# Four edits to a decoder step on eight cores: order of the first loads, spills as rows are done, conv weights in halves, all last down tiles segment by segment

## The reference, cut to what matters

```python
def decoder_layer(x, ...):
    x = x + 0.5 * swiglu_ffn(rms_norm(x, ffn1_norm), ffn1_w_gu, ffn1_w_down)
    mix, ... = token_mixer(rms_norm(x, mix_norm), conv_prev, ...)
    x = x + mix
    x = x + 0.5 * swiglu_ffn(rms_norm(x, ffn2_norm), ffn2_w_gu, ffn2_w_down)
# swiglu_ffn: gate, up = split(x @ w_gu); (silu(gate) * up) @ w_down
# rms_norm:   x * rsqrt(mean(x*x) + eps) * g
# token_mixer: spatial gating branch + (GLU, depthwise conv of width 31, layer norm, silu) branch, gated, one output projection
y = rms_norm(x, final_norm)
```

## Time and profile before

| | us |
|---|---|
| median of 3 runs | 3295.9 (3292.66 to 3832.61) |
| the profiled execution | 3292.83 |
| its span, first to last instruction, slowest core (7) | 3291.3 |
| spans of the eight cores | 3272.9 to 3291.3 |
| PE busy | 3188.5 (97%) |
| DVE busy | 1303.8 (40%) |
| ACT busy | 518.5 (16%) |

### The profile page before, as it was taken

One profiled execution on the slowest core, in us unless ns is written; L12 is line 12 of the kernel. 1 busy time (PEld: TensorE's weight loads), 2 busy tenths in 40 slices (PEclk: granted clock), 3 DMA queues, 4 the chain that ended last, 5 costly groups with the idle time before them and its releaser, 6 DMA issues.

```text
span 3291.3 us, 52487 instructions; the slowest of 8 cores (3272.9 to 3291.3 us)
## 1 busy us (share of the span) xinstructions
PE 3188.5 (97%) x21434; PEld 2052.3 (62%) x21434; DVE 1303.8 (40%) x2368; ACT 518.5 (16%) x957; POOL 128.1 (4%) x246
## 2 busy tenths in 40 slices
PE   6999999999999899999999999999999999999995
PEld 3566666666666576688666666666666666666662
DVE  2433333333336476675642222234333333333345
ACT  2200100000015122245111011033100100100121
POOL 0000000000000000000000000000000000000000
PEclk7999999999999899999999999999999999999997
DMA  6435624335336655534434433482434334434333
GB/s 164 77 58 102 108 52 84 70 56 89 70 62 163 120 115 119 120 82 93 87 56 78 77 70 64 73 186 52 90 62 86 68 59 86 73 59 81 72 62 109
DMA packets 75213, 284.38 MB, mean 86 GB/s; under 512 B 10977, under 2 KB 37857, under 8 KB 53090
## 3 DMA queue, kind: packets, MB, share of 16 engines
q0 software_dynamic: 34848, 216.62, 37.4%
q1 hardware_dynamic: 40130, 64.41, 6.7%
HBM read 468.13 MB, written 32.89 MB: 152 GB/s over the span
## 4 chain that ended last, share of the span: by engine, by line
PE 93%; DMA 3%; DVE 3%; issue 1%; ACT 1%; DVEq 0%; SPq 0%; ACTq 0%; POOLq 0%
PE ps L201 93%; DVE arena L207 1%; DVE arena L214 1%; DMA arena<-xin 1%; DMA cst<-arena 1%; DMA arena<-xsp 1%; DMA arena<-w_glu 1%; DMA arena<-w_gu 1%; DVE arena L218 0%; ACT arena L204 0%; ACT L204 0%; DVE arena L210 0%; DVEq L1138 0%; DVE arena L221 0%; SPq L1147 0%
## 5 line engine op out<-in xcount | busy, mean ns | idle before, releaser
L201 PE MATMUL ps<-arena 128*128 128x384 bf16 (+5 forms) x21434 | 3188.5, 311 | 88.7 <-ACT arena L204 26.3
L201 PEld LDWEIGHTS ps<-arena 128*128 128x128 bf16 x21434 | 2052.3, 98 | 1224.6 <-issue 115.8
L204 ACT ACTIVATE arena<-arena 128x384 f32<-128x384 f32 (+7 forms) x780 | 412.0, 550 | 2563.1 <-DVE arena L207 2405.8
L207 DVE TENSOR_TENSOR arena<-ps,arena 128x384 f32<-128x384 f32 (+2 forms) x504 | 270.4, 538 | 774.7 <-PE ps L201 752.9
L207 DVE TENSOR_TENSOR arena<-arena 128x384 f32<-128x384 f32 (+12 forms) x682 | 461.0, 688 | 283.0 <-ACT arena L204 249.5
L214 DVE SCALAR_TENSOR_TENSOR arena<-ps,arena 128x384 f32<-128x384 f32 (+6 forms) x452 | 241.7, 537 | 414.9 <-PE ps L201 414.1
L207 DVE TENSOR_TENSOR arena<-arena,ps 128x384 bf16<-128x384 f32 (+6 forms) x488 | 225.9, 477 | 393.7 <-PE ps L201 374.0
L1147 POOL DMA_DIRECT2D arena<-w_gu x88 | 46.6, 530 | 1160.2 <-PE ps L201 1131.7
L204 ACT ACTIVATE arena<-ps,arena 128x272 bf16<-128x272 f32 (+4 forms) x148 | 69.8, 487 | 134.8 <-PE ps L201 131.2
L1147 POOL DMA_DIRECT2D arena<-w_dn x64 | 33.8, 528 | 772.4 <-PE ps L201 772.4
L218 DVE RECIPROCAL arena<-arena 128x384 f32<-128x384 f32 (+4 forms) x14 | 36.6, 2613 | 51.3 <-ACT arena L204 51.3
(11 more groups left out here) (9 smaller groups left out, 8.0 us busy)
## 6 DMA issues: line engine op xcount, KB each, us to landing
arena<-w_gu POOLq DMA_DIRECT2D x88, 1024.0 KB, 9.2
arena<-w_dn POOLq DMA_DIRECT2D x64, 704.0 KB, 7.2
arena<-w_glu POOLq DMA_DIRECT2D x16, 1024.0 KB, 10.1
arena<-w_gate POOLq DMA_DIRECT2D x16, 1024.0 KB, 9.0
arena<-w_pab POOLq DMA_DIRECT2D x16, 1024.0 KB, 10.1
arena<-w_v POOLq DMA_DIRECT2D x8, 1024.0 KB, 8.8
arena<-w_u POOLq DMA_DIRECT2D x8, 1024.0 KB, 8.0
arena<-w_out POOLq DMA_DIRECT2D x8, 1024.0 KB, 11.1
```

The costliest lines, as they stand in the source:

```text
L201: return P.op("pe", lambda e: e.matmul(out, lhsT, rhs, start=start, stop=stop), deps)
L204: return P.op("act", lambda e: e.activation(out=out, in_=in_, func=func, **kw), deps)
L207: return P.op("dve", lambda e: e.tensor_tensor(out=out, in0=in0, in1=in1, op=op), deps)
```

## The change

What it does:

1. *Prelude.* All four loads of segment 0 are issued at once. The hook is called before a weight tile is issued and gives a wait for it: tile 1 waits for segment 0's group 2, tile 2 for segment 1's group 1, tile 3 for segment 2's group 0. Segment 1's loads wait for segment 0's last one, segment 2's for segment 1's last. In `units_by_row` the gate parts of all tiles come before the up parts.
2. *Spill.* Rows 0 to 3, 4 to 7 and 8 to 9 are stored as soon as they are done (hook "m"), rows 10 to 15 as before.
3. *Conv weights.* Each is a list of two halves, run one after each `glu_unit`; the memsets and the first weights stand behind block 0 of the held blocks.
4. *Last group of the second FFN.* `dn_seg` is 8: all eight down tiles are held and run segment by segment. Four are in the slots, four more go to `spare`, the place of H2, by DMAs on POOL that wait for the last gate/up matmul. `direct` is 12 for segment 0 and 6 for the others (before: 10).
5. *Final norm.* ACT multiplies X by the gain in place behind each row's Square. `finish` only does `root`; `last_rows` gives four steps, each one DVE tensor_tensor of 4 rows (128x1536 or 128x1280) by RSTD and the store of these rows. Segment s - 1's steps run behind rows 2, 4, 6 and 8 of segment s, the last segment's at the end.

```diff
@@ -266,7 +266,7 @@
 ev_pv = P.dma("sp", PV, pv_d, "c_pv")
-load_tokens(0, (0, 1))
+load_tokens(0, range(4))
@@ -327,7 +327,10 @@
         self.pend.append((k, si, sq[:, 0:n], act(sq[:, 0:n], X, AF.Square, deps=[dep] + sfree)))
-        if self.Hout is not None:
+        if self.Hout is None:
+            self.out[(self.s, k)] = act(X, X, AF.Identity, deps=[self.pend[-1][3], ev_pv],
+                                        scale=pvc(self.gidx, k))
+        else:
@@ -360,24 +363,31 @@
-    def finish(self, on_pool=()):
+    def finish(self):
         self.flush()
-        er = root(self.bank, self.lm, self.x0, self.n)
-        self.rout[self.s] = er
-        if self.Hout is None:
-            n, s = self.n, self.s
-            for k in range(KC):
-                X = self.Xs[s][:, k, 0:n]
-                R = RSTD[:, self.x0:self.x0 + n]
-                self.out[(s, k)] = stt(X, X, pvc(self.gidx, k), R, ALU.mult, ALU.mult, deps=[er, ev_pv],
-                                       eng="dve")
+        self.rout[self.s] = root(self.bank, self.lm, self.x0, self.n)
+    def last_rows(self):
+        if self.Hout is not None:
+            return []
+        x0, n, s = self.x0, self.n, self.s
+        def rows(g):
+            def run():
+                X = self.Xs[s][:, 4 * g:4 * g + 4, 0:n]
+                e = tt(X, X, RSTD[:, x0:x0 + n].unsqueeze(1).to_broadcast([128, 4, n]), ALU.mult,
+                       deps=[self.rout[s], self.out[(s, 4 * g + 3)]])
+                P.dma("sp", y_o[:, 4 * g:4 * g + 4, x0:x0 + n], X, "o_y", deps=[e])
+            return run
+        return [rows(g) for g in range(4)]
...
-def ffn(segs, Hv, HID, Xs, hready, rstd, norms, dn_seg, x_final, hook, first):
+def ffn(segs, Hv, HID, Xs, hready, rstd, norms, dn_seg, x_final, hook, first, spare=()):
@@ -429,8 +439,9 @@
         tok.finish()
-        for (jj, slot, lev), ((gi_, bg, _f), (ui_, bu, _h)) in zip(tiles, got):
-            up_part((ui_, bu), last[jj][1], jj, s, gate_part((gi_, bg), last[jj][0], s))
+        gps = [gate_part((gi_, bg), last[jj][0], s) for (jj, slot, lev), ((gi_, bg, _f), _u) in zip(tiles, got)]
+        for (jj, slot, lev), (_g, (ui_, bu, _h)), gp in zip(tiles, got, gps):
+            up_part((ui_, bu), last[jj][1], jj, s, gp)
@@ -450,11 +461,10 @@
                 if not wahead:
-                    wissue()
+                    wissue(hook("w", jj))
                 held.append(wnext())
-                hook("w", jj, held[jj][2])
             if not wahead:
-                wissue()
+                wissue(hook("w", 3))
@@ -485,12 +495,20 @@
             wdone(wi, [ld])
+            if gi == 3:
+                hook("m", mp)
...
             for mp in range(nm, 8):
-                held.append((mp,) + wnext())
+                if len(held) < 4:
+                    held.append((mp,) + wnext())
+                else:
+                    src, n = wseq.pop(0)
+                    buf = spare[len(held) - 4]
+                    held.append((mp, None, buf, P.dma("pool", buf, src, "wx%d" % mp, deps=norms[0].hdep)))
             for s in range(3):
+                steps = norms[s - 1].last_rows() if s > 0 else []
@@ -502,9 +520,12 @@
                         if s > 0 and m == 16 - 2 * dn_seg:
-                            norms[s - 1].finish(range(8, 16))
-                    if s == 2:
+                            norms[s - 1].finish()
+                        elif m % 2 == 0:
+                            run_steps(steps, 1)
+                    if s == 2 and wi is not None:
                         wdone(wi, [ld])
+                run_steps(steps, 99)
@@ -521,7 +542,9 @@
     if what == "w":
-        load_tokens(i, (2, 3) if i == 0 else range(4), [ev])
+        if i in (1, 2):
+            load_tokens(i, range(4), [x_ev[(i - 1, 3)]])
+        return [] if i == 0 else [x_ev[((0, 2), (1, 1), (2, 0))[i - 1]]]
@@ -546,15 +569,13 @@
         cst["wp"] = P.dma("pool", WP, wp_d, "c_wp")
-    if what == "g" and i == 3:
-        m1 = 16 - 2 * DN_SEG
+    if what == "m" and i % 2 == 1 or what == "m" and i == 7 - DN_SEG:
+        m0, m1 = 4 * (i // 2), 2 * i + 2
         for s in range(3):
-            sp_ev[(s, 0)] = P.dma("sp", xsp[s][:, 0:m1, :], X1[s][:, 0:m1, :], "xsa%d" % s,
-                                  deps=[x1f[(s, m1 - 1)]])
+            P.dma("sp", xsp[s][:, m0:m1, :], X1[s][:, m0:m1, :], "xsp%d" % s, deps=[x1f[(s, m1 - 1)]])
     if what == "s":
-        m1 = 16 - 2 * DN_SEG
-        sp_ev[(i, 1)] = P.dma("sp", xsp[i][:, m1:16, :], X1[i][:, m1:16, :], "xsb%d" % i,
-                              deps=[x1f[(i, 15)]])
+        m0 = 16 - 2 * DN_SEG
+        sp_ev[i] = P.dma("sp", xsp[i][:, m0:16, :], X1[i][:, m0:16, :], "xsp%d" % i, deps=[x1f[(i, 15)]])
@@ -655,23 +676,29 @@
 def conv_weights(c):
-    wp = WP[:, c]
-    e = None
-    for h in range(2):
-        e = tt(WD[c % 2][:, 2 * h:2 * h + 2].rearrange("p g b (i c) -> p (g b i) c", c=32),
-               MSKC.unsqueeze(1).to_broadcast([128, 72, 32]),
-               wp[:, 72 * h:72 * h + 72].unsqueeze(2).to_broadcast([128, 72, 32]), ALU.mult,
-               deps=[cst["wp"]] + wd_free[c % 2] + x1_dead)
-    return e
+    def half(h):
+        def run():
+            built[c] = h + 1
+            cw[c] = tt(WD[c % 2][:, 2 * h:2 * h + 2].rearrange("p g b (i c) -> p (g b i) c", c=32),
+                       MSKC.unsqueeze(1).to_broadcast([128, 72, 32]),
+                       WP[:, c, 72 * h:72 * h + 72].unsqueeze(2).to_broadcast([128, 72, 32]), ALU.mult,
+                       deps=[cst["wp"]] + wd_free[c % 2] + x1_dead)
+        return run
+    build.extend([half(0), half(1)])
+build = []
+built = {}
+cw = {}
...
 cg = {}
-cw = {}
 def conv(c):
+    while c not in cw or built[c] < 2:
+        run_steps(build, 1)
@@ -732,21 +759,24 @@
                 x1_dead = [hm[(0, 15)], hm[(1, 15)], hm[(2, 15)]] + list(sp_ev.values())
+                e_ph = memset(PHM, 0.0, deps=x1_dead)
+                for i in range(4):
+                    e_ph = memset(PHM[32 * i:32 * i + 32, i, :], 1.0, deps=[e_ph])
+                conv_weights(0)
+                conv_weights(1)
+            else:
+                run_steps(build, 1)
...
     cg[c] = conv_cache(c)
-e_ph = memset(PHM, 0.0, deps=x1_dead)
-for i in range(4):
-    e_ph = memset(PHM[32 * i:32 * i + 32, i, :], 1.0, deps=[e_ph])
-cw[0] = conv_weights(0)
-cw[1] = conv_weights(1)
...
         la = glu_unit(c, slot, lev, s)
+        run_steps(build, 1)
@@ -756,7 +786,7 @@
         if cc + 2 < KC:
-            cw[cc + 2] = conv_weights(cc + 2)
+            conv_weights(cc + 2)
@@ -1102,20 +1132,17 @@
 yf = {}
-normf = [RowNorm(PV_FIN, X2, None, SEG_B, s, yf, {}, SQF, ACCF[s], 10, PARTS[s]) for s in range(3)]
+normf = [RowNorm(PV_FIN, X2, None, SEG_B, s, yf, {}, SQF, ACCF[s], (12, 6, 6)[s], PARTS[s]) for s in range(3)]
...
-ffn(SEG_B, H2, HID2, X2, h2, r2, normf, 3, x3f, hook2,
+spare = [view(OFF_US + i * 5632, [2816], BF16) for i in range(4)]
+ffn(SEG_B, H2, HID2, X2, h2, r2, normf, 8, x3f, hook2,
     [(0, [0], None, norm2[2].finish), (0, [1, 2], None, None), (1, [0, 1, 2], None, None),
-     (2, [0, 1, 2], None, None)])
-normf[2].finish(range(11, 16))
-for s in range(3):
-    x0, n = SEG_B[s]
-    for g in range(4):
-        P.dma("sp", y_o[:, 4 * g:4 * g + 4, x0:x0 + n], X2[s][:, 4 * g:4 * g + 4, :], "o_y",
-              deps=[yf[(s, 4 * g + q)] for q in range(4)])
+     (2, [0, 1, 2], None, None)], spare)
+normf[2].finish()
+run_steps(normf[2].last_rows(), 99)
```

More of the change, by code:

```diff
@@ L211, in ts, with stt @@
                                                          op0=op0, op1=op1), deps)
-        def stt(out, in0, scalar, in1, op0, op1, deps=(), eng="dve"):
-            return P.op(eng, lambda e: e.scalar_tensor_tensor(out=out, in0=in0, scalar=scalar, in1=in1,
+        def stt(out, in0, scalar, in1, op0, op1, deps=()):
+            return P.op("dve", lambda e: e.scalar_tensor_tensor(out=out, in0=in0, scalar=scalar, in1=in1,
                                                                 op0=op0, op1=op1), deps)
@@ L1058, in build_program @@
                                     xsp[s][:, 4 * mg:4 * mg + 4, 0:SEG_B[s][1]], "xr%d_%d" % (s, mg),
-                                    deps=[lya, lyb, lgb, sp_ev[(s, 0)], sp_ev[(s, 1)]])
+                                    deps=[lya, lyb, lgb, sp_ev[s]])
         x2f = {}
```

## The result

The changed kernel takes 3258.2 us (median of 4 runs, 3257.5 to 3258.85) against 3294.3: a ratio of 0.9892, 95% interval 0.9873 to 0.9912. It is 36 us faster, 1.1%, where 46.9 us (1.4%) were forecast. That is less than the 2% which the forecast took as the mark of a change, as it said; by the interval it is a gain.

The account below looks back on a forecast made before the run. The prediction took the kernel as bound by matmuls (PE busy 3188.5 of 3291.3 us). 18.8 + 3.4 + 6.5 + 18.2 = 46.9 us off 3292.8 gave 3246, 3249 for the median; range 3236 to 3267, its own 3238 to 3258.

Parts of the forecast that it names:

- rival B: Prelude bound by the chain of loads, tile 1 at 36 us or later: 10 us less gain, 3259; chance 0.18.
- C: Rival: a new wait at the end, from late extra tiles or DVE falling further behind: 3257 to 3265; chance 0.17.
- Part 1: Prelude: reordered loads 17.5 us, gate products ahead of ups about 1.3 us; 18.8 us off.
- the chain: Prelude: tile 0 near 15 us, segment 0 in at 21.5, tile 1 near 30.5, PE goes on at 38.6.
- Part 2: Spill: without the store burst ahead of the GLU tiles, 2 us less wait and 1.4 of slow matmuls; 3.4 off.
- Part 3: Conv weights: wait of 9.35 us ahead of the first block falls by 6.2, cool-down by 0.3; 6.5 off.
- the cores draw together: Conv weights: the slowest core gets this gain and the quickest less; no size given.
- Parts 4 and 5: Last group and final norm: PE's waits of 2.95, 11.56 and 10.56 us go, smaller ones come; 18.2 us off.
- The extra tiles: Last group: four more down tiles land at 11.5 to 24.5 us, just in time, so no wait.
- E: Rival: the extra tiles cost more than everything else gives, from 47 us of wait on them; chance 0.02.
- The tail: Kernel's end: four steps replace 16 products, so stores start earlier; 1.1 to 1.9 us off.
- Each restart: PE's matmuls behind a long wait run partly at the lower clock level: 1.5 us charged each time.

Follow-up runs that it names:

- e2: The kernel before with the spill's edit alone (rows 0 to 9 stored as they are done): ratio 0.9988.
- e7: The changed kernel with the last of three GLU tiles held until the second has landed: ratio 0.9888 to the kernel before.
- e5: The changed kernel with one more half of the conv weights built behind conv block 1: 3252.9 us.
- e8: The changed kernel with weight tile 1 waiting for segment 0's second load instead of its third: ratio 0.9882 to the kernel before.

## Why the prediction was right, and where it was wrong

**Direction, verdict and range**: right, 3258.2 lies in 3236 to 3267, at the edge of the forecast's own range of 3238 to 3258. The size was 1.3 times the measured one, and 9.7 of the 10.8 us of difference lie in one place, the middle. The time alone would speak as well for rival B (3259) or C (3257 to 3265); the lines speak against both, as tile 1 came before 36 and the last group has no wait over 3.4 us.

**Part 1, right in the chain and the total, in part by luck.** 18.8 forecast, 17.7 measured (14.2 on core 3). The chain was as worked out: first load at 8.1 us, segment 0 in at 22.7, tile 1 behind the third load. But each step came later than in the sum, tile 0 at 17.6 in place of 15, and segment 1's by-row start at 40.6 in the mean over the cores, not 38.6: 14.6 us earlier than before, not 17.5. What made up for it was no term of the sum: the 112 matmuls behind that start took 18.36 us, where they had taken 20.3 in the mean (granted clock 1.00 on core 3, 0.89 on core 7 before). POOL's timeline of the changed kernel, core 3:

```profile
21.35 0.53 POOL L1174 DMA_DIRECT2D arena<-w_gu  x1 [19.13 <-DMA arena<-xin]
38.81 0.53 POOL L1174 DMA_DIRECT2D arena<-w_gu  x1 [16.93 <-DMA arena<-xin]
```

Tile 1 was issued at 21.35, not 18.5, and took 12.4 us; the sum had 12. On core 6 it was issued at 19.58 and PE started on it at 30.25. The Trainium skill's formula ("DMA: Bandwidth & Descriptors", section "Anatomy of one DMA"), from which an estimate of 4.4 us follows for a tile of this size, fails again here: the tiles of the prelude took 10.5 to 15.8 us on cores 3 and 6, with X beside them. The wait of 4.98 us that the order of the gates was to shorten by 1.3 is 3.70: 1.28.

**Part 2, wrong: 3.4 forecast, none measured.** The failed step is "The stores of rows 0 to 9 no longer come in one burst just ahead of three GLU tiles, whose third load holds PE". They do end earlier, and it changes nothing (e2: 2.12 and 2.13 us in the mean). The tile's own queue is a part of the cause: with the third of three tiles held back until the second had landed, the wait for w_glu fell on core 3 from 3.09 to 2.11 us (e7). The rest stays open.

**Part 3, wrong by a wait that was costed at nothing.** The first wait went from 9.35 us on core 7, the slowest before, to 1.82 on core 3, the slowest after (forecast 6.2 off, to about 3.2, behind gd): right in kind and place on the cores that had it. But not every core did. The kernel before, cores 3 and 1:

```profile
1137.63 275.19 PE L201 MATMUL ps<-arena 128*128 128x256 bf16 x2432 [9.96 <-DVE arena L207]
1126.04 273.62 PE L201 MATMUL ps<-arena 128*128 128x256 bf16 x2432 [1.56 <-DMA arena<-gd]
```

On cores 0, 3, 5 and 7 the wait was 8.8 us in the mean and is now 0.2 to 2.0; over all eight it was 6.1 and is 1.2, so 4.9 us is what this edit had to give the table's middle. The main failed step is "two halves fit into a block of 15.6 us three times over: free". I counted DVE's time per block, and for most blocks that is right; but the order {3: [0], 4: [1, 2], 5: [3, 4]} runs two conv blocks behind one GLU block twice, and at the second there are four halves for three units. It costs 4.3 us on every core, which leaves 0.6 of the 4.9, and e5 gives it back, 5.3 in time. Nor did the cores draw together as forecast: their spans were 18.4 us apart and are 16.1.

**Parts 4 and 5, right.** 18.2 forecast, 17.5 measured (the sum's own numbers, 3277.1 less 3259.4 or 3260.7, give 16.4 to 17.7 for PE's part, where it says 17.1). The waits: 3.8 and 3.45 forecast, 3.35 and 3.40 measured. The wide products of the changed kernel (count, busy us, mean ns):

```profile
L207 DVE TENSOR_TENSOR arena<-arena 128x1536 f32<-128x1536 f32 x8 | 14.0, 1752 | 0.0
...
L207 DVE TENSOR_TENSOR arena<-arena 128x1280 f32<-128x1280 f32 x4 | 5.7, 1488 | 0.1
```

1.76 and 1.5 us were the terms. The extra tiles (w_dn from 3120 to 3200 us, six issues, landing):

```profile
L1174 POOL DMA_DIRECT2D arena<-w_dn x6: 527/542/568, 3129.9 to 3146.7; - x6
...
DMA to landing us min/median/max: 6.9/11.3/19.0
```

The latest of them landed 19.0 us after its issue, where 24.5 was the estimate and 25 the need: rival C's and E's condition was not there, as PE has no wait on w_dn. The tail gave 0.5 us, not 1.1 to 1.9 (14.5 to 14.0 from PE's last matmul to the end): the last product is done at 3250.99, 5.0 us ahead of the end, and the four last stores run at 327 to 371 GB/s in all but their first and last slice (GB/s in 40 slices of 3236 to 3257 us), so they, not the products, set it.

```profile
GB/s 0 0 0 0 0 0 0 0 0 0 0 0 0 0 0 0 0 0 0 0 0 0 202 368 327 361 368 346 351 356 368 327 363 371 358 356 171 0 0 0
...
y<-arena SPq DMA_DIRECT2D x4, 640.0 KB, 4.0
```

ACT is busy 28.1 us longer, not 22: the 32 instructions of 384 columns that came in took 0.61 us each (178.0 us of this form less 158.5 before), where the sum had 0.47. PE waits behind ACT for 1.9 us in the whole kernel, so it cost little. Each restart was charged 1.5 us; the one behind the wait of 4.3 us cost 1.4 to 2.1 (2432 matmuls in 275.04 and 275.70 us on cores 5 and 0 of the changed kernel, 273.62 on the four cores of e5 where they ran through behind waits of 0.3 to 2.3).

## What to carry to other kernels

A queue of small deferred jobs, run one at each step of a loop, has to be counted where the loop's steps are fewest for the jobs that fall due, not per step on average: here one stretch with four jobs and three steps took back 4.3 of the 4.9 us that the wait before had fallen by in the mean over the cores. A wait that is read on one core should be read on all of them before it is priced: this one was 9.35 us on the slowest and 6.1 in the mean. When a load is waited for, the stores on another queue that are easiest to move need not be the cause: moving 5.9 MB of them changed nothing here, and holding back a later tile of the same queue took 0.8 us off the mean wait and nothing off the time. A partial sum that is handed from DVE to PE should be split where DVE has caught up, not soonest: moving it from rows 12, 6 and 6 to 15, 15 and 13 was worth 10 us and one line.

## What the runs showed that was not expected

The cores go in pairs. Of cores 0 and 1, 2 and 3, 4 and 5, 6 and 7, in the changed kernel one waits 3.1 to 3.5 us for w_glu and the other not at all; in e8 one waits 2.9 to 4.0 us and the other not at all. PE's timeline of core 6 (its long run from 1034 to 1153 has no wait) and of core 7:

```profile
1033.92 119.48 PE L201 MATMUL ps<-arena 128*128 128x384 bf16 x924 [0.34 <-DVE arena L207]
1157.72 225.95 PE L201 MATMUL ps<-arena 128*128 128x256 bf16 x1952 [4.32 <-DVE arena L207]
```

```profile
1059.99 53.10 PE L201 MATMUL ps<-arena 128*128 128x384 bf16 x320 [3.34 <-DMA arena<-w_glu]
1114.47 4.99 PE L201 MATMUL ps<-arena 128*128 128x256 bf16 x72 [1.38 <-DMA arena<-gd]
```

The one that comes later through the prelude (core 7 starts its long run at 91.2 us, core 6 at 87.9) gets the waits, in e8 too, and the distance grows. Which of the two it is changes from one execution to the next. The spans are

```profile
core 0: 3241.6 us, clock 0.992
core 1: 3253.9 us, clock 0.992
core 2: 3241.4 us, clock 0.992
core 3: 3256.0 us, clock 0.990
core 4: 3255.1 us, clock 0.991
core 5: 3244.6 us, clock 0.992
core 6: 3239.9 us, clock 0.993
core 7: 3252.9 us, clock 0.991
```

In each pair the spans differ by 10 to 15 us, while the prelude left 2 to 5. A saving on the core that is ahead is worth nothing to the metric, and one that shifts a core against its neighbour can cost as much as it gives, which may be why e7 and e8 won nothing; no run here tried the two cores of a pair apart.
